# Split mixer projections, a six-slot weight ring, and a reordered RWKV start in a two-layer hybrid backbone

## The reference

```
h = adaLN(RMSNorm(x))                        # scale and shift from SiLU(c) @ ada_w
P = h @ W_in                                 # RWKV 1920, RetNet 2048, HGRN2 2560, gates 3072 columns
RWKV:   p += mu * (shifted - p)              # mean of neighbours: sequence (context), 4x64 grid (latent)
        r, k, v, decay, a, g; layer 1: v += (v_first - v) * sigmoid(v0 + (h @ v_down) @ v_up)
        delta-rule state in chunks of 64, forward and backward, 8 heads of 64
RetNet: rope(q), rope(k), decay-masked q k^T, times v; 4 heads of 128
HGRN2:  lower-bounded gates, chunks of 128, 4 heads of 128
x += gate1 * (sum_b sigmoid(P_gate_b) * (Y_b @ W_branch_b)) @ W_out
x += gate2 * relu(h2 @ W1)^2 @ W2 ;  after both layers: RMSNorm of the latent half
```

## Time and profile before

| | |
|---|---|
| median of 3 runs | 2741.78 us (2738.88 to 3275.7) |
| profiled execution | 2744.85 us, its span 2743.1 us |
| granted TensorE clock, mean | 0.943 |
| PE busy | 2462.0 us (90%) |
| PEld / DVE / ACT / POOL busy | 68% / 43% / 34% / 16% |
| HBM read | 230.62 MB, 86 GB/s over the span |

### The profile page before, as it was taken

One profiled execution on the slowest core, in us unless ns is written; L12 is line 12 of the kernel. 1 busy time (PEld: TensorE's weight loads), 2 busy tenths in 40 slices (PEclk: granted clock), 3 DMA queues, 4 the chain that ended last, 5 costly groups with the idle time before them and its releaser, 6 DMA issues.

```text
span 2743.1 us, 54656 instructions
## 1 busy us (share of the span) xinstructions
PE 2462.0 (90%) x23538; PEld 1856.9 (68%) x23538; DVE 1178.4 (43%) x1831; ACT 923.2 (34%) x1308; POOL 437.1 (16%) x455
## 2 busy tenths in 40 slices
PE   4988989898999889998999989888879898898998
PEld 1553748494855568876888856466857766598998
DVE  2323444444423343445444433254453523366665
ACT  3323232223234332334223342332232334345554
POOL 0002221212123310001000000132231314400000
PEclk8999999899999989998999989999989999899999
DMA  7313322313011023332233232200000012055553
GB/s 277 126 51 117 133 73 77 115 35 147 3 62 54 35 85 96 100 123 70 92 97 95 92 125 77 71 18 25 3 24 10 18 44 73 35 177 196 157 179 103
DMA packets 64031, 239.38 MB, mean 87 GB/s; under 512 B 7088, under 2 KB 8240, under 8 KB 62512
## 3 DMA queue, kind: packets, MB, share of 16 engines
q1 hardware_dynamic: 61920, 218.13, 24.0%
q10 hardware_dynamic: 1872, 17.75, 1.6%
HBM read 230.62 MB, written 5.24 MB: 86 GB/s over the span
## 4 chain that ended last, share of the span: by engine, by line
PE 79%; DVE 8%; ACT 6%; POOL 3%; issue 2%; DMA 2%; ACTq 0%; DVEq 0%; SPq 0%; POOLq 0%
PE psum L411 13%; PE psum L384 11%; PE psum L386 11%; PE psum L385 11%; PE psum L398 10%; PE psum L758 7%; PE psum L420 2%; PE psum L762 2%; PE psum L483 2%; PE psum L720 2%; PE psum L658 1%; POOL work L1799 1%; ACT L1383 1%; PE psum L447 1%; DMA work<-in_ret_constants 1%
## 5 line engine op out<-in xcount | busy, mean ns | idle before, releaser
L398 PE MATMUL psum<-normed,weight_ring 128*128 128x512 f32 (+1 forms) x864 | 372.5, 589 | 33.4 <-ACT normed L1437 12.6
L398 PEld LDWEIGHTS psum<-normed,weight_ring 128*128 128x128 f32 x864 | 176.5, 209 | 225.8 <-issue 210.2
L411 PE MATMUL psum<-work 64*64 64x64 f32 (+1 forms) x9088 | 307.7, 222 | 14.9 <-ACT work L1618 10.5
L929 DVE TENSOR_TENSOR weight_ring_parts<-weight_ring,weights_high 128x1024 fp32r<-128x1024 f32 (+1 forms) x224 | 266.7, 1191 | 125.5 <-ACT weights_high L1398 121.1
L411 PEld LDWEIGHTS psum<-work 64*64 64x64 f32 x9088 | 294.7, 135 | 26.6 <-issue 15.6
L385 PE MATMUL psum<-normed_low_part,weights_high 128*128 128x512 f32 (+1 forms) x896 | 304.1, 339 | 0.0
L1398 ACT ACTIVATE weights_high<-weight_ring 128x1024 fp32r<-128x1024 f32 (+1 forms) x224 | 230.8, 1030 | 160.5 <-PE psum L386 149.0
L758 PE MATMUL psum<-normed,weight_ring 128*128 128x512 f32 (+1 forms) x512 | 200.6, 539 | 2.7 <-ACT work L1383 2.7
L384 PE MATMUL psum<-normed_high,weights_high 128*128 128x512 f32 (+1 forms) x512 | 178.3, 348 | 15.6 <-DVE normed_low_part L917 15.2
L385 PEld LDWEIGHTS psum<-normed_low_part,weights_high 128*128 128x128 f32 x896 | 173.3, 193 | 21.3 <-issue 0.5
L386 PE MATMUL psum<-normed_high,weight_ring_parts 128*128 128x512 f32 (+1 forms) x512 | 176.9, 346 | 0.0
(11 more groups left out here) (241 smaller groups left out, 4218.6 us busy)
## 6 DMA issues: line engine op xcount, KB each, us to landing
weight_ring<-in_weights SPq DMA_DIRECT2D x406, 512.0 KB, 3.6
x_scratch<-work ACTq DMA_DIRECT2D x2, 2048.0 KB, 7.4
weight_ring<-in_weights SPq DMA_DIRECT2D x16, 256.0 KB, 2.8
work<-x_scratch ACTq DMA_DIRECT2D x2, 2048.0 KB, 10.3
work<-in_ret_constants ACTq DMA_DIRECT2D x2, 1152.0 KB, 12.7
work<-in_small_weights ACTq DMA_DIRECT2D x2, 1152.0 KB, 5.2
work<-in_x ACTq DMA_DIRECT2D x1, 2048.0 KB, 14.8
constants<-in_constants ACTq DMA_DIRECT2D x1, 1315.0 KB, 9.1
```

What stands on the lines that cost most here:

```text
L398: last = mm(ps[:, 0:t1 - t0], tiled(s, k), hT[:, k, t0:t1], start=(k == 0), stop=(k == KT - 1))
L411: last = mm(ps[q, w * m:w * m + w], lhs(q, m), rhs(q, m), start=True, stop=True)
L929: tt(ring_r[:, i % RING, o], ring[:, i % RING, o], high[:, n % HIGHS, o].bitcast(F32), ALU.subtract).then_inc(vec_split.sem, vec_split.ste ...
```

## The change

- `RING` 9 to 6, `HIGHS` 4 to 3. The room goes to `normed_high`, now a buffer of its own instead of a place in the work area, kept from the first norm to the gates.
- All mixer projections (`mixer_order`: retention, small, RWKV, HGRN; 51 slots in layer 0, 52 in layer 1) join `split_order` and are multiplied by `rounded`. Each gets a `weights_high` on ACT and a `weights_low` on DVE, placed at points of their programs. POOL makes the high part of h after norm 1 (as after norm 2), DVE the remainder; the separate split for the gates goes.
- Retention values of all four heads are computed first, from four slots `rv`, with the weights as the moving operand of width 512 (`tokens_out`); HGRN's `hi` likewise. Retention and HGRN results go to the four `dense` banks instead of two. `freed` now knows what holds a bank across pools, and waits for that.
- Layer 1's v_down becomes a fourth small slot. `v_first` is saved to DRAM after RWKV of layer 0 and brought back after HGRN, since `keys_of_a_level` now lies on it.
- The modulation products spread out: one behind k of the retention heads 0, 1 and 2, and one each at "kk", "values", "level1", "level3" of every RWKV pair in layer 0.
- Mixing: ACT writes the raw values and also the own part, scaled; DVE adds the side neighbours and does the weighted sums; POOL adds the vertical (and sequence) neighbours alone.
- DVE reads `gb` and `gk` of direction 0 before it mixes v; in layer 1 the gate of v follows the first level; the bonus terms move to j == 2. A copy of 8 columns becomes a multiply by one.
- In the dense stages `AHEAD` + 1 becomes `HIGHS`: the split runs one tile nearer to the tile just finished.

```diff
-RING = 9
-HIGHS = 4
+RING = 6
+HIGHS = 3
...
+            def project(pool, filled, w, key, t0=0, tiles=range(KT)):
+                if 0 in tiles:
+                    pool.fill(*key)
+                    for free in pool.freed():
+                        eng.wait_ge(*free)
+                ps = pool.get(*key)[:, 0:N - t0]
+                for k in tiles:
+                    last = rounded(ps, w, (normed_hi[:, k, t0:N], hT_r[:, k, t0:N]), k, k == 0, k == KT - 1)
...
@@ PE, retention
+                for q in range(4):
+                    tokens_out("rv", split("rv", l, q), l, q, range(4), True)
...
+                        project(dense, dense_filled, split("ret", l, c, 0), ("rq", l, c), lo)
+                        project(dense, dense_filled, split("ret", l, c, 1), ("rk", l, c))
+                        modulation("rk", l, c)
+                        project(dense, dense_filled, split("ret", l, c, 2), ("rg", l, c), lo)
...
@@ DVE
+                weights_low(split_at["rv", l, 2])
                 tail(l, 1)
+                weights_low(split_at["ret", l, 0, 1] + 1)
 
                 for h in range(4):            # the strips, unchanged
...
-                    if what == "P" and c == 0:
-                        modulation("strips", l)
+                    if what == "P":
+                        weights_low(split_at["ret", l, c, 2] + 1)
+                        modulation("rk", l, c)
...
@@ DVE, mix
+                    tt(sides.rearrange("p (r t) -> p r t", t=GRID), grid[:, 1:5, 0:64], grid[:, 1:5, 2:66], ALU.add)
+                    eng.wait_ge(act_rwkv.sem, act_rwkv.at("own part", l, i))
+                    stt(dst[:, NC:N], sides, dcol(D_QMU + i), dst[:, NC:N], ALU.mult, ALU.add)
+                    eng.wait_ge(pool_rwkv.sem, pool_rwkv.at("neighbours", l, i))
...
@@ DVE, scores of direction d
                         tt(chunks(B + ABT, m0=m0), ps[:, m0:, 64:128], ...)          # gb read
+                        if d == 1:
+                            first_level(0)
+                            if l > 0:
+                                values_gated()
                         eng.wait_ge(wide_filled.sem, wide_filled.at("gk", l, c, d))
...
+                        if d == 0:
+                            values()
+                    first_level(1)
...
@@ ACT, start and retention
+                if l == 0:
+                    weights_high(HIGHS)
                 norm(l, 1)
...
+                            weights_high(split_at["ret", l, c, i] + HIGHS + 1)   # behind reading rq, rk
...
@@ ACT and DVE, MLP (gates and output alike)
-                        weights_high(split_at["m1", l, f] + AHEAD + 1)
+                        weights_high(split_at["m1", l, f] + HIGHS)
-                        weights_low(split_at["m1", l, f] + AHEAD + 1)
+                        weights_low(split_at["m1", l, f] + HIGHS)
```

More of the change, by code:

```diff
@@ L139, in schedule_slots @@
         ada("start", l)
[L140 to L154, removed]
+        for key in split_order(l):
+            out.append(key)
+            if key[0] == "ret" and key[3] == 1:
+                ada("rk", l, key[2])
+            if key[0] == "rw" and key[3] == 2:
+                for name in ("kk", "values", "level1", "level3"):
+                    ada(name, l, key[2])
+            if key == ("ga", l, 0, 2):
+                ada("out", l)
     return out
@@ L389, in tiled @@
                 return s[:, k * P:(k + 1) * P]
[L391 to L396, removed]
-                        eng.wait_ge(act_norm.sem, act_norm.at("h tile", key[1], after_norm, k))
-                    last = mm(ps[:, 0:t1 - t0], tiled(s, k), hT[:, k, t0:t1], start=(k == 0), stop=(k == KT - 1))
-                last.then_inc(big_filled.sem, big_filled.step(key))
+            def project(pool, filled, w, key, t0=0, tiles=range(KT)):
[6 more added lines that the diff above has]
+                    last = rounded(ps, w, (normed_hi[:, k, t0:N], hT_r[:, k, t0:N]), k, k == 0, k == KT - 1)
+                if KT - 1 in tiles:
+                    last.then_inc(filled.sem, filled.step(key))
@@ new lines, in tokens_out @@
+            def tokens_out(name, w, l, q, tiles, after_norm=False):
+                for i in tiles:
+                    if q == 0:
+                        dense.fill(name + " tile", l, i)
+                        for free in dense.freed():
+                            eng.wait_ge(*free)
+                    ps = dense.get(name + " tile", l, i)
+                    t = slice(P * i, P * i + P)
+                    for k in (2 * q, 2 * q + 1):
+                        if after_norm and i == 0:
+                            eng.wait_ge(vec_mlp.sem, vec_mlp.at("normed split", l, 1, k))
+                        c = slice(BW * (k % 2), BW * (k % 2) + BW)
+                        mm(ps, normed_hi[:, k, t], w[0][:, c], start=(k == 0), stop=False)
+                        mm(ps, normed_hi[:, k, t], w[1][:, c], start=False, stop=False)
+                        last = mm(ps, hT_r[:, k, t], w[0][:, c], start=False, stop=(k == KT - 1))
+                if 3 in tiles:
+                    last.then_inc(dense_filled.sem, dense_filled.step((name, l, q)))
@@ L1877, in _ @@
                         branch_high(b, k)
[L1878 to L1883 removed]
+                normed_high(2, t0, t1)
         @block.sync
```

474 lines of the change are left out of this document (258 added, 216 removed), and 9 rows, old and new, of the table ADA_AT.

## The result

The changed kernel takes **2694.8 us** (median), the kernel before 2741.4 in the same comparison: ratio **0.9829** (95% interval 0.9809 to 0.9848), 1.7% faster. The forecast was 2643 us, 3.6% faster. The time lies inside the forecast's range, but the gain is under half of what was worked out. The profiled execution spans 2687.0 us against 2743.1. The 3275.7 us in the table of the kernel before is one slow execution, and no ratio contains it.

A forecast was written before the change was run, and what follows sets the result against it. PE, busy 90% of the span, was taken as the bound. Projections -118, RWKV start -60, small projections -7, strips +37, start +12, lead +28 and HGRN +9 sum to -99, forecasting 2643 us, range 2580 to 2705.

The forecast's parts named there:

- The projections: Mixer projections of both layers: rounded steps shorten tiles of 512 and 256 columns and retention values, -118 us in sum.
- The path from k to the first level: RWKV pairs: the new order shortens this stretch from 57.4 to 44 us in layer 1, 68.5 to 56 in layer 0, levels' 6 included.
- The strips: Retention: PE waits for rg's low part behind DVE's strips loop, 21 us in layer 0, 18 in layer 1; +37 net.
- The lead in layer 1's gates: Gates of layer 1: splitting one tile later makes PE wait 1.75 us at each of eight gates, 14 us.
- the lower -60: RWKV start, both layers: 76 us of gain worked out, 30 if DVE and POOL contend; -60 taken.
- Start: Start and norms: a later norm 1 (4.7 us) and the parts of h (2.7 per layer) delay first matmuls; +12 in sum.
- Mixing: RWKV pairs: fewer POOL instructions ahead of the last sums save 2.5 us for k and 1.5 for r.
- HGRN: 20 splits per layer on ACT and DVE: layer 0 has room, layer 1 loses 13 us, stage end gains 4; +9.
- Lead in the MLP: MLP of layer 1: PE waits 0.35 to 0.4 us in each of 32 up tiles, 11 us.
- Contention in HGRN: Rival, chance 0.15: each of 40 low parts collides with a POOL step of 1.26 us, RWKV gains only 30; 2723 us.
- the lead costs nothing: Rival, chance 0.17: ring and lead suffice everywhere, strips wait half as long; 2597 us, 2581 with all of RWKV's 76.
- the reorder does nothing: Rival, chance 0.09: the first RWKV level still waits for POOL's b terms, so RWKV gains only 10; 2693 us.

The follow-up runs named there:

- no_products_before: The kernel before without the 16 modulation products of layer 0's RWKV pairs and what follows from them: ratio 0.9870, 2705.5 us.
- ring6_before: The kernel before with a ring of six slots, three high parts and one tile less of lead, nothing else changed: ratio 1.0264, 2818.7 us.
- lead_back: The changed kernel with weights split one tile further ahead in gates, output, up and down projections: ratio 0.9755, 2678.0 us.
- order_alone: The kernel before with only DVE's order of drains in RWKV changed (ACT's sigmoid for v's gate moves along): ratio 0.9855, 2707.5 us.
- strips: The changed kernel with one line moved, so DVE subtracts three low parts ahead of its strips loop: ratio 0.9706, 2664.8 us.
- banks: The changed kernel with the PSUM bank count shifted by two before each layer's first HGRN projection: ratio 0.9797, 2685.7 us.
- mended: The changed kernel with four cures together: low parts before strips, more lead, shifted banks, ACT's third high part behind norm 1's squares: ratio 0.9649, 2649.1 us.

## Why the prediction was wrong, and what of it held

**What held.** The projections: PE's busy time fell by 124.6 us against 118. The path from k to the first level in the two pairs whose rows I had: 46.9 and 50.0 against 44 and 50. The strips: 20.6 and 18.1 against 21 and 18, and the cure by one line. The lead in layer 1's gates: 12.8 against 14. Layer 1's pairs as a stage: -38 against -44. That the time lies in the range says little, since the range reached up to no gain in RWKV at all; a time within 2% had been given 0.19.

**The step that failed** is the sentence "In layer 0 the same stretch has 68.5 us ... so 12.5 less ... Four pairs each". It took one pair for four and priced what moves into the levels at its own 6 us. The four pairs of layer 0 (us, before and after; the last ends at HGRN):

| pair | k to first level | first level to next k | sum |
|---|---|---|---|
| 0 | 65.4, 50.9 | 60.7, 71.2 | 126.1, 122.1 |
| 1 | 64.6, 51.2 | 62.1, 69.5 | 126.7, 120.8 |
| 2 | 68.5, 50.0 | 61.8, 68.6 | 130.3, 118.5 |
| 3 | 63.5, 50.0 | 60.6, 77.7 | 124.1, 127.7 |

Worked out were 18.5 less in the first column and 6 more in the second, in every pair: 50 us in all, of which the lower -60 for both layers left 44. It came to 18. The first column gave 60 instead of 74, because I had read the pair with the longest start. The second took 42 instead of 24. Of these 18 us some 13 are the waits without a releaser that the products bring among the levels, and 5 the bank at HGRN's entry, which falls into the last pair. (One execution each; a pair can differ by 5 us between executions.)

The runs agree. The order of the drains removes a wait for DVE, and in layer 0 that wait wasn't there to remove: modulation products stood in front of it and hid 39 us in all (no_products_before). Alone, the order gave 31 us in layer 1 and 8 in layer 0. The products, moved into the values and the levels, cost 16 us more than at their old places (each of the two comparisons is good to some 7). My note on the levels ("PE has no gap and pays their 6 us") measured 7 in the second pair, but 10.5 in the first and 12 in the last without the bank; what I didn't see is that the old place had been paid for by a wait, and that the new one brings waits of its own.

**Terms that were mis-sized.** *Start:* 15.4 us against 8. The ring of six in the opening modulation is 12.9 of it (ring6_before shows it by itself), the parts of h 2.1 against 3.7 counted, and ACT's splits ahead of the squares under 2 against 4.7. The ring I had checked in RWKV ("I cost it at nothing in RWKV") and not where the waits for weights already were the earlier trace rows. *Mixing:* counted as 32 us in all, worth 20. *Retention of layer 0:* 9 us more, of which 6.0 is the low part of a later rg behind a rotation, the same fault as at the strips, of which I had found one; 1.3 is a longer wait for the last rotation (8.2 against 6.9). The other 2 are no wait that the list shows; PE's granted clock in the stage fell from 0.96 to 0.87 (below), and I put them to that without a run of its own. *HGRN:* "Layer 0 has room" was wrong by 6.6 us; layer 1's splits cost 9.4 against 13. (The 237 us of the earlier trace rows also held 22 us of the gates, which begin at 966.25.) Its entry: PE waits 6.1 and 5.2 us behind the last gate product, where the kernel before waited 1.3 and 1.5 behind ACT. In layer 0 that is a bank; for layer 1 it is not shown. Nothing in the working had looked at which bank a stage begins with. *Lead in the MLP:* 4.4 against 11, so the estimate of 0.35 us a tile was 0.14.

**The rivals.** Contention in HGRN came in kind, not in size. That the lead costs nothing is refuted by lead_back, that the reorder does nothing by order_alone. The way the kernel went, gains that were smaller than in the one pair read and were partly taken back at places not listed, was in none of them.

## What to carry to other kernels

Before a wait is counted as a gain in every turn of a loop, look at it in every turn: work that happens to stand in front of it may hide it, and moving that work away uncovers both. After the move, price the new place too: here it brought idle time that the moved work's own length didn't contain. When a buffer ring is made smaller, go first to the place where the profile already waits for it, and count which loads stand back to back. Preparing work for PE belongs ahead of an engine's long stretches, not behind them: one line moved was worth more than most terms here, and the cures that worked were cheap once the wait had a name.

## What the runs showed of the hardware

- An operation on the last column of each chunk (128 x 8) takes 1.11 us as a multiplication by ones, as the copy took 1.12; I had counted 1 us for getting rid of the copy. Its length is not that of its 8 columns: 504 columns beside it take 0.68.
- The same instructions don't take the same time from pair to pair: in kernels whose RWKV of layer 0 is identical (changed, strips, lead, banks, mended) the stretch from gb of pair 2 to gb of pair 3 took 117.0 to 122.8 us. A difference of 5 us in one stage of one profile is no evidence.
- PE is slower behind waits. In the stage of layer 0's retention and in HGRN of layer 1 (us, PE, PEld, DVE, ACT, POOL, granted clock, DMA share, GB/s), before and after:

```profile
52.89:211.74 158.85, 144.45 (x537) 79.78 (x537) 48.38 (x80) 51.95 (x77) 4.15 (x4) 0.96 0.26 91
...
2223.23:2394.14 170.91, 150.77 (x553) 94.62 (x553) 49.50 (x94) 70.71 (x113) 68.30 (x78) 0.97 0.19 60
```
```profile
68.31:244.21 175.90, 132.97 (x521) 93.82 (x521) 74.11 (x104) 68.16 (x92) 10.12 (x11) 0.87 0.30 106
...
2156.28:2320.86 164.58, 136.82 (x712) 118.33 (x713) 77.99 (x101) 85.82 (x127) 72.14 (x70) 0.91 0.19 63
```

The granted clock falls from 0.96 to 0.87 and from 0.97 to 0.91. Behind the wait of 20.6 us the rounded matmuls repeat every 0.43 us (128.52, 128.95), at the lower of the two levels, against 0.23 in the earlier trace rows. So in HGRN of layer 1 PE's busy time shrank by 14 us, where its tiles were worth 20 (8 x 0.61 + 12 x 1.27), and the stage by 6.3: it looks as if a stage that PE no longer fills gives part of its gain back in clock, beside its waits. No run separates the two.
